# Routing by token tile, compression in column halves, and block 1's side work in another order

## The chip, the cores and the metric

The kernel runs on one core of a Trainium2 chip. The metric is the device time of one execution in microseconds (us); a profiled execution has its own time beside it. The engines are TensorE (PE, with its weight loads PEld), VectorE (DVE), ScalarE (ACT), GpSimd (POOL) and SyncE (SP), which issues most transfers.

## The reference, cut to what matters

The input x has 256 tokens of 1024 features. A first block and two further layers follow one another, all in float32.

```python
# block 1
h = rms_norm(x, g);  z = h @ w_in              # fox q,k,v,f; nsa q and keys/values; gates
out_a = fox_attention(q, k, v, log_sigmoid(f + b)) @ w_fox_up        # 8 heads of 64
kc, vc = gelu(blocks @ w1) @ w2                # compression of keys and of values, each its own w1, w2
out_b = nsa_attention(compressed, selected, window branches) @ w_nsa_up
x = x + (sigmoid(g_a) * out_a + sigmoid(g_b) * out_b) @ w_out
# experts: top group of 4, then top 2 of its 4 experts
t = rms_norm(x, g_ffn)
p_g, group = top_k(softmax(t @ w_group + b_group), 1)
top_p, top_i = top_k(softmax((t @ w_router + b_router)[group]), 2)
x = x + sum(w * (silu(t @ w_gate[e]) * (t @ w_up[e])) @ w_down[e])
# two layers: HGRN2 recurrence and sliding-window attention, post-norm, residual
for l in range(2): x = x + rms_norm(mixed(rms_norm(x, g_pre)) @ w_out_2[l], g_post)
```

## The kernel before, in words

Every large product is computed in float32r with both operands split into a high and a low part: three matmuls (`mm3`, hi*hi, hi*lo, lo*hi, the lines 507 to 509). Weights stream from memory in halves of 1 MB through a ring of four slots. Each half is four pieces of 512 columns; ScalarE writes a piece's high part (`feed`, line 1766), VectorE its low part (line 398), into nine buffers. PE eats two pieces per "take". Both engines run their feeds nine pieces ahead (`AHEAD`); a buffer is free when the take that used it has counted `taken`. Each engine runs its own written program, and semaphores with `wait_ge` join them. What an engine does besides the takes stands in a table by take number (`beside_block1`, `beside_layer`): a `step` is run by each engine `ahead` of or `behind` its part of the take.

Takes 0 to 23 compute z for block 1, four takes for 512 columns: tile a=0 of the tokens goes to bank 0, a=1 to bank 1. After each fourth take ScalarE copies bank 0 and VectorE bank 1 to `z3` (VectorE's line 1689), and PE's next take waits for both (`out_free`). In between run the head norms (`fox_sums`, `fox_norms`, `win_sums`, ...: VectorE squares and sums, GpSimd takes the root), the turns (transposes) of queries and keys (`fox_q`, `fox_k`, `nsa_side`), the forget gates (`forget`, whose end stands in VectorE's `fox_q`), and twelve attention jobs. A job has the steps scores, `scores_out` (VectorE mask and maxima, ScalarE exponentials), `weigh` (VectorE), turn, `turn_out`, values, `values_out`. Takes 24 to 39 are gates, 40 to 47 the up projections, 48 to 55 the output projection. Beside takes 28 to 42 run the thirteen steps of `compress`. Its steps 3 and 4 multiply keys' blocks and then values' blocks by w1 (line 711), each into partitions 0 to 63 of bank 7, 256 columns side by side; the four raw halves of w1 sit in the ring.

Takes 48 to 55 fill banks 4 to 7. Then VectorE adds the result to x, `norm(1)` squares (ScalarE, line 1780), takes the root (GpSimd), scales, PE turns x into feature rows with the gain applied on the way out (ScalarE and VectorE, eight copies each), and `route` computes 20 logits per token (`mm3` with 20 columns), softmax and choice of the group, ranks of tokens within their group (lines 786 to 790), eight selection matrices of 128 slots (`sel_r`), and the gather of each group's rows (line 805). If a group has more than 128 tokens, all engines but GpSimd run `full_pass`; the flag for it is read to a register by each engine (`value_load`, `If`), on PE ahead of the gather. In the run shown no group was so crowded. After the gather PE spreads the expert weights to slots (line 811), ScalarE and GpSimd split the rows (`expert_rows`), and 192 expert takes follow, 48 a group. `combine` adds the groups' results back, and the layers follow, with `pre_sum`, `pre_scale` and `pre_los` ahead of each and `y_sums`, `y_add` at its end.

Of the kernel before, what the change touches and what calls it, by code (L numbers as in the profile page):

```python
# [98 lines left out]
def weight_halves():  # L99
# [4 lines left out]
    for n in range(PN_CMP):  # L104
        for h in range(2):
            out.append((2 * n + h, PIECE if n != 2 else Z5, engines))
            if n == 8 and h == 1:
                out += [(2 * PN_CMP + i, 0, None) for i in range(2)]
            if n == 9 and h == 0:
                out += [(2 * PN_CMP + 2 + i, 0, None) for i in range(2)]  # L110
# [113 lines left out]
def build(nc, panels, x_in, prm_in, lay_in, pre_in, post_in, c0_in, c1_in, c2_in, out):  # L224
    ctx = ExitStack()
    with ctx:
# [96 lines left out]
        def sem(name):  # L323
# [12 lines left out]
            sem("norm_" + n) for n in ("sq", "ms", "rs", "x", "T", "hi", "lo"))  # L336
        x_new = sem("x_new")
# [4 lines left out]
        route_hi, route_lo = sem("route_hi"), sem("route_lo")  # L342
# [90 lines left out]

# [28 lines left out]
        full_x, full_w, full_g, full_hT = zin[:, 4096:5120], gates[:, :], buf_d[:, 1024:1536], buf_d[:, 1536:2048]  # L463
# [41 lines left out]
        def pe_program():  # L505
# [111 lines left out]
            def nsa_side(n):  # L617
                c, kind = SIDES[n]
                pe.wait_ge(heads_done, (3, 4, 3, 5)[n])
                if n == 0:  # L620
                    pe.wait_ge(norm_lo, 8)
                else:
                    pe.wait_ge(side, 5 + n)
                if kind == "q":
                    pair_turns(c, 7, z3).then_inc(side_T, 1)
                    return
                for a in range(TT):
                    i = turn128(ps[:, 7, a * P:(a + 1) * P], z3[:, a, c:c + P])
# [63 lines left out]
            def compress(step):  # L692
# [10 lines left out]
                elif step < 5:  # L703
                    c = step - 3
                    pe.wait_ge(cmp_blk, 8)
                    for h in range(2):
                        load = raw_at[2 * c + h]
                        pe.wait_ge(*landed(load))
                        w1 = ring[:, load % RING * HALF:(load % RING + 1) * HALF].rearrange("p (m n) -> p m n", m=8)
                        for n in range(8):  # L710
                            m = T.matmul(ps[0:64, 7, c * 256:(c + 1) * 256], blk[c][:, 8 * h + n, :, :].rearrange("p g n -> p (g n)"),  # L711
                                         w1[:, n, :], start=h == 0 and n == 0, stop=h == 1 and n == 7)
                elif step == 5:
                    pe.wait_ge(cmp_a, 1)
                    for i in range(4):
                        m = turn128(ps[:, 7, i * 64:(i + 1) * 64], scr[0:64, i * P:(i + 1) * P], 64)
                elif step == 6:
                    pe.wait_ge(cmp_v, 3)
                    pe.wait_ge(ld_prm, 16)
                    for c in range(2):  # L720
                        w2 = prmc(("w2_k", "w2_v")[c])
                        for i in range(2):
                            m = T.matmul(ps[0:64, 7, c * 64:(c + 1) * 64],
                                         scr[:, 512 + (2 * c + i) * 64:512 + (2 * c + i + 1) * 64],
# [51 lines left out]

            def route():
                pe.wait_ge(route_lo, 1)
                for a in range(TT):
                    for k in range(KT):  # L780
                        pe.wait_ge(norm_lo, 8 + k + 1)
                        m = mm3(ps[:, 0, a * 20:(a + 1) * 20], (hi3[:, k, a * P:(a + 1) * P], lo3[:, k, a * P:(a + 1) * P]),
# [3 lines left out]
                T.matmul(ps[:, 1, 0:4], ntri[:, 0:P], goh2[:, 0:4], start=True, stop=True)  # L786
                T.matmul(ps[:, 1, 4:8], ntri[:, P:2 * P], goh2[:, 0:4], start=True, stop=False)
                T.matmul(ps[:, 1, 4:8], ntri[:, 0:P], goh2[:, 4:8], start=False, stop=True)
                T.matmul(ps[:, 1, 8:12], ntri[:, P:2 * P], goh2[:, 0:4], start=True, stop=False)
                T.matmul(ps[:, 1, 8:12], ntri[:, P:2 * P], goh2[:, 4:8], start=False, stop=True).then_inc(rank_mm, 1)  # L790
# [6 lines left out]
                pe.wait_ge(chosen, 8)  # L797
                pe.wait_ge(rs_lo, 4)
                for k in range(KT):
                    if k >= 4:  # L800
                        pe.wait_ge(rows, k - 3)
                    b = 3 + k % 4
                    for x in (op_hi, op_lo):
                        for a in range(TT):
                            m = T.matmul(ps[:, b, :], x[:, a * D + k * P:a * D + (k + 1) * P], sel_r[:, a * 512:(a + 1) * 512],  # L805
                                         start=a == 0 and x is op_hi, stop=a == 1 and x is op_lo)
                    m.then_inc(row_mm, 1)
# [57 lines left out]
            def full_pass():  # L865
                for a in range(TT):
# [142 lines left out]
            for t in range(T_OUT, T_MOE):  # L1009
                k = t - T_OUT  # L1010
                pe.wait_ge(mix_lo, k // 2 + 1)
                out_take(t, op_rows, k, k == 0, k == KT - 1)
            norm_turns(1)
            route()
            for t in range(T_MOE, T_L2):
                expert(t)
                if t - T_MOE in SELECT_AT:
# [30 lines left out]
        def dve_program():  # L1048
# [49 lines left out]
            def fox_sums(n):  # L1098
                for a in range(TT):
                    dve.wait_ge(out_free[a], 2)  # L1100
# [1269 lines left out]
```

## Time and profile before

| what | us |
|---|---|
| median of 3 runs | 1128.57 (1127.06 to 1132.99) |
| the profiled execution | 1132.04 |
| its span, first to last instruction | 1130.2 |
| PE / VectorE / ScalarE / GpSimd busy | 1049.0 / 851.0 / 657.0 / 50.4 |
| mean granted clock of PE | 0.964 |

Busy times overlap, and PE counts as busy while matmuls are in its pipeline. The granted clock is 1.00 at 2.4 GHz and 0.50 at 1.2 GHz.

### The profile page before, as it was taken

The page shows a single profiled execution, that of the slowest core. Times are in us where ns is not written, and L with a number is a line of the kernel's source. Part 1 is how long each engine was busy: PE and PEld are TensorE (multiplying, and loading weights), DVE is VectorE, ACT ScalarE, POOL GpSimd, SP SyncE. Part 2 cuts the span into 40 slices and gives each one's busy share as a digit, 9 for nine tenths or more (in the row PEclk, how much of TensorE's full clock was granted, in tenths as well). Part 3 has the DMA queues.
Part 4 walks back from the last instruction along what each step waited for, and adds up shares of the span by engine and source line. Part 5 has one row for each costly group of instructions (what it writes and reads, how often), then busy time and mean ns, then how long its engine had stood idle before and what let it go on. Part 6 is the DMA issues. An engine that isn't in the chain of part 4 may idle for free.

```text
span 1130.2 us, 16492 instructions
## 1 busy us (share of the span) xinstructions
PE 1049.0 (93%) x6109; PEld 896.4 (79%) x6109; DVE 851.0 (75%) x1663; ACT 657.0 (58%) x1314; POOL 50.4 (4%) x44
## 2 busy tenths in 40 slices
PE   4898999897799999999989999999998999989997
PEld 4776878787588888887877898888876899978875
DVE  5666774674599999999986777697567877598673
ACT  5443545543488888888863566822345467653342
POOL 0201100000100101020000000000001000000010
PEclk9998999997699999999999999999998999999999
DMA  8422335242099999999973433323343533333320
GB/s 345 158 112 75 113 131 197 86 179 80 7 373 382 362 387 358 384 368 347 373 284 133 172 125 125 114 104 140 121 162 132 185 129 134 113 112 113 126 98 38
DMA packets 30036, 211.32 MB, mean 187 GB/s; under 512 B 3584, under 2 KB 3712, under 8 KB 4992
## 3 DMA queue, kind: packets, MB, share of 16 engines
q1 hardware_dynamic: 28368, 205.01, 48.8%
q10 hardware_dynamic: 1584, 5.20, 1.3%
q8 instruction: 52, 0.85, 0.3%
q14 instruction: 32, 0.26, 0.1%
HBM read 209.15 MB, written 1.05 MB: 186 GB/s over the span
## 4 chain that ended last, share of the span: by engine, by line
PE 64%; DVE 20%; ACT 7%; DMA 5%; issue 3%; POOL 0%; SPq 0%; DVEq 0%; POOLq 0%; ACTq 0%
PE ps L507 16%; PE ps L509 15%; PE ps L508 15%; DVE w_lo L398 9%; DMA ring<-in_panels 5%; PE ps L512 4%; PE ps L942 4%; PE ps L657 2%; ACT w_hi L1766 2%; PE ps L688 1%; PE ps L711 1%; ACT s_buf L1814 1%; DVE scr L398 1%; PE ps L805 1%; DVE op_lo L398 1%
## 5 line engine op out<-in xcount | busy, mean ns | idle before, releaser
L398 DVE TENSOR_TENSOR w_lo<-ring,w_hi 128x512 fp32r<-128x512 f32 x760 | 482.6, 689 | 108.8 <-ACT w_hi L1766 107.6
L1766 ACT ACTIVATE w_hi<-ring 128x512 fp32r<-128x512 f32 x760 | 426.2, 620 | 194.1 <-PE ps L509 161.8
L507 PE MATMUL ps<-w_hi,op_hi 128*128 128x512 f32 (+2 forms) x800 | 320.2, 400 | 19.5 <-ACT zin L1766 5.0
L509 PE MATMUL ps<-w_hi,op_lo 128*128 128x512 f32 (+2 forms) x800 | 312.9, 391 | 0.0
L508 PE MATMUL ps<-w_lo,op_hi 128*128 128x512 f32 (+2 forms) x800 | 312.4, 391 | 0.0
L507 PEld LDWEIGHTS ps<-w_hi,op_hi 128*128 128x128 f32 x800 | 154.2, 193 | 54.6 <-issue 10.4
L509 PEld LDWEIGHTS ps<-w_hi,op_lo 128*128 128x128 f32 x800 | 153.7, 192 | 31.6
L508 PEld LDWEIGHTS ps<-w_lo,op_hi 128*128 128x128 f32 x800 | 154.4, 193 | 28.0
L507 PE MATMUL ps<-op_hi,w_hi 128*128 128x256 f32 x544 | 157.5, 290 | 1.2 <-DVE op_lo L398 1.2
L508 PE MATMUL ps<-op_lo,w_hi 128*128 128x256 f32 x544 | 153.8, 283 | 0.0
L509 PE MATMUL ps<-op_hi,w_lo 128*128 128x256 f32 x544 | 153.7, 283 | 0.0
L507 PEld LDWEIGHTS ps<-op_hi,w_hi 128*128 128x128 f32 x544 | 104.0, 191 | 5.2 <-issue 2.5
L508 PEld LDWEIGHTS ps<-op_lo,w_hi 128*128 128x128 f32 x544 | 104.2, 191 | 0.0
L509 PEld LDWEIGHTS ps<-op_hi,w_lo 128*128 128x128 f32 x544 | 104.1, 191 | 0.0
L1814 ACT ACTIVATE s_buf<-s_buf,stat 128x256 f32<-128x256 f32 (+1 forms) x112 | 49.6, 444 | 73.2 <-DVE stat L401 73.2
L410 POOL TENSOR_TENSOR stat<-stat,minus_half 128x1 f32<-128x1 f32 (+5 forms) x20 | 25.9, 1296 | 842.8 <-DVE stat L404 842.8
L942 PEld LDWEIGHTS ps<-gates 128*128 128x128 f32 x448 | 54.3, 192 | 5.5 <-issue 3.3
L942 PE MATMUL ps<-gates 128*128 128x64 f32 x448 | 53.3, 271 | 3.0 <-DVE buf_c L1572 3.0
L512 PE MATMUL ps<-ident,scr 128*128 128x128 f32 (+3 forms) x109 | 18.9, 329 | 26.7 <-DVE scr L401 20.6
L512 PEld LDWEIGHTS ps<-ident,scr 128*128 128x128 f32 (+3 forms) x109 | 15.8, 170 | 29.3 <-issue 14.4
L1766 ACT ACTIVATE zin<-ps 128x512 f32<-128x512 f32 (+2 forms) x26 | 14.0, 554 | 38.6 <-PE ps L509 24.3
L398 DVE TENSOR_TENSOR gates<-gates,buf_d 128x512 f32<-128x512 f32 (+1 forms) x36 | 25.5, 746 | 13.3 <-PE ps L942 13.3
(244 smaller groups left out, 1131.2 us busy)
## 6 DMA issues: line engine op xcount, KB each, us to landing
ring<-in_panels SPq DMA_DIRECT2D x194, 1024.0 KB, 6.1
cst<-in_c ACTq DMA_DIRECT2D x1, 1219.0 KB, 5.4
buf_a<-in_pre ACTq DMA_DIRECT2D x2, 512.0 KB, 5.9
keys<-in_post ACTq DMA_DIRECT2D x2, 512.0 KB, 4.5
out<-x_tok SPq DMA_DIRECT2D x2, 512.0 KB, 2.6
cst<-in_c ACTq DMA_DIRECT2D x1, 960.0 KB, 7.0
x_tok<-in_x SPq DMA_DIRECT2D x1, 512.0 KB, 4.8
x_tok<-in_x ACTq DMA_DIRECT2D x1, 512.0 KB, 5.0
```

Of the source, the lines that this page charges most:

```text
L398: return V.tensor_tensor(o, a, b, op)
L410: return G.tensor_tensor(o, o, e.to_broadcast(list(o.shape)), ALU.pow)
L507: T.matmul(o, l[0], r[0], start=start, stop=False)
L508: T.matmul(o, l[0], r[1], start=False, stop=False)
L509: return T.matmul(o, l[1], r[0], start=False, stop=stop)
L512: return T.transpose(o, a, ident[0:n, 0:n])
L657: m = T.matmul(ps[:, 2 + e, lo:lo + n], q(a)[half, :], k[half, 0:n], start=True, stop=plain)
L688: m = T.matmul(ps[half, 6, kt * P:S], v3[:, kt, cc:cc + HD], pt[:, kt * S:S + kt * P], start=kt == 0, stop=kt == 1)
L711: m = T.matmul(ps[0:64, 7, c * 256:(c + 1) * 256], blk[c][:, 8 * h + n, :, :].rearrange("p g n -> p (g n)"), w1[:, n, :], start=h == 0 and ...
L942: m = T.matmul(ps[:, 2 + 2 * j + lv % 2, n * HD:(n + 1) * HD], k_of(j)[:, n * P:(n + 1) * P], late[:, n * per:(n + 1) * per, :], start=Tru ...
L1766: return A.activation(o, a, ACT.Copy, scale=scale)
L1814: i = A.activation(sc[:, lo:lo + n], sc[:, lo:lo + n], ACT.Exp, bias=ng_[:, c:c + 1], accum_out=sm[:, c:c + 1])
```

## The change

- `last_takes_1`: the last four output takes run all of tile a=0 and then all of a=1. Squares, root, scaling, turns, splitting and logits are done per tile. The gain `g_ffn` is multiplied into the router's weights once (in `lower`), so that the turned rows need none. The rows to be gathered are split from `scr` into `pick_hi`, `pick_lo`.
- In `route`, the group's sum and reciprocal come after its choice; ranks take two products; the gather starts at four selections and goes through four banks for a=0 and then a=1. ScalarE copies rows and splits expert rows in turn. The branch comes behind the gather on PE and ScalarE. The slot weights move behind the third expert take, their copy behind the fifth.
- VectorE feeds pieces 115 to 118 inside `route`, behind the selections.
- Compression: steps 3 and 4 each take a half of w1 for keys and values, keys to partitions 0 to 63 and values to 64 to 127. Step 8 is cut in two (`cmp_weigh`), and the weighings of jobs 7 and 11 come ahead (`weigh_now`).
- Block 1: new places in the table; bank copies ahead of the feed (VectorE) and ahead of the exponentials (ScalarE); `forget` ends in VectorE's `fox_k`; `nsa_side` 1 uses bank 3.
- `combine` and tails: tile a=0 is summed and scaled ahead of a=1's sums; mean and epsilon come from one instruction; one feed stands ahead of the combine.

```diff
-    table = {4: [("lower", 0)], 9: [("fox_sums", 0)], 10: [("fox_sums", 1)], 11: [("fox_norms", 0), ("forget", 0)],
-             12: [("fox_norms", 1), ("fox_q", 0), ("nsa_gates", 0)], 13: [("fox_k", 0)],
-             20: [("win_sums", 0)], 21: [("win_norms", 0), ("nsa_side", 0)], 22: [("nsa_side", 1)],
+    table = {3: [("lower", 0)], 5: [("fox_sums", 0)], 7: [("fox_norms", 0)], 9: [("fox_sums", 1), ("fox_q", 0)],
+             11: [("fox_norms", 1), ("forget", 0)], 12: [("fox_k", 0), ("nsa_gates", 0)],
+             20: [("win_sums", 0)], 21: [("win_norms", 0)], 22: [("nsa_side", 0), ("nsa_side", 1)],
...
+    for take, job in ((31, 7), (39, 11)):
+        table[take].remove(("weigh", job))
+    table[30].insert(table[30].index(("compress", 2)), ("weigh_now", 7))
+    table[38] += [("weigh_now", 11), ("cmp_weigh", 0)]
...
+                    for n in range(8):
+                        for c in range(2):
+                            m = T.matmul(ps[c * 64:(c + 1) * 64, 7, 0:256],
+                                         blk[c][:, 8 * h + n, :, :].rearrange("p g n -> p (g n)"),
+                                         w1[c][:, n, :], start=h == 0 and n == 0, stop=h == 1 and n == 7)
...
+            def last_takes_1():
+                for a in range(TT):
+                    for k in range(KT - 4, KT):
+                        w = weights_of(T_MOE - KT + k)
+                        pe.wait_ge(mix_lo, k // 2 + 1)
+                        for h in range(2):
+                            m = mm3(ps[:, 4 + 2 * a + h, :], op_rows(k, a), w[h], False, k == KT - 1)
+                        if a == 1:
+                            m.then_inc(taken, 1)
+                    if a == 0:
+                        m.then_inc(ffn_mm, 1)
...
+                for a in range(TT):
+                    for c in range(2):
+                        pe.wait_ge(ffn_x, 2 * a + c + 1)
+                        for i in range(4):
+                            o = a * D + (4 * c + i) * P
+                            m = turn128(ps[:, 2 + 2 * a + c, i * P:(i + 1) * P], scr[:, o:o + P])
+                        m.then_inc(ffn_T, 1)
                     for k in range(KT):
-                        pe.wait_ge(norm_lo, 8 + k + 1)
+                        pe.wait_ge(ffn_lo, 2 * a + k // 4 + 1)
...
+                for k0 in (0, 4):
+                    for a in range(TT):
+                        pe.wait_ge(chosen, 4 * (a + 1))
+                        for k in range(k0, k0 + 4):
+                            if k0 and a == 0:
+                                pe.wait_ge(rows, k - 3)
+                            for y in (pick_hi, pick_lo):
...
                 pe.wait_ge(flagged, 1)
                 more = T.value_load(flag[0:1, 0:1], min_val=0, max_val=S)
                 with T.If(more > 0):
...
+            ffn_sum(0)
+            ffn_scale(0)
+            feed(2 * (T_MOE - 3) + AHEAD)
+            ffn_sum(1)
+            ffn_lo_(0)
+            ffn_scale(1)
+            pick_los(0)
+            ffn_lo_(1)
+            pick_los(1)
             route()
```

## Rows read from the trace of the kernel before

**Rows 1.** Windows by stage: length, busy us (instructions) of each engine, clock, DMA share, GB/s

```profile
264.43:307.11 42.68, 28.05 (x122) 25.74 (x123) 18.96 (x72) 17.59 (x33) 1.56 (x3) 0.60 0.02 4
307.11:587.65 280.54, 280.20 (x1255) 229.53 (x1256) 266.87 (x427) 238.27 (x443) 19.20 (x15) 0.99 0.96 365
```

**Rows 2.** Timeline, PE in block 1: start, us, instruction [idle before <-releaser]

```profile
51.37 0.80 PE L507 MATMUL ps<-w_hi,op_hi 128*128 128x512 f32 x1 [3.62 <-DVE zin L1689]
...
71.09 0.47 PE L507 MATMUL ps<-w_hi,op_hi 128*128 128x512 f32 x1 [2.49 <-ACT zin L1766]
...
109.45 0.48 PE L512 MATMUL ps<-ident,zin 128*128 128x128 f32 x1 [2.30 <-DVE zin L398]
...
156.21 0.87 PE L512 MATMUL ps<-ident,s_buf 128*128 128x128 f32 x6 [2.49 <-DVE s_buf L401]
...
211.57 1.40 PE L512 MATMUL ps<-ident,s_buf 128*128 128x128 f32 x6 [2.66 <-DVE s_buf L401]
```

**Rows 3.** Windows, the stretch behind the first hole

```profile
51.33:54.74 3.41, 3.37 (x10) 2.69 (x11) 1.55 (x4) 1.73 (x4) 1.75 (x1) 0.50 0.00 0
```

**Rows 4.** Timeline, VectorE and ScalarE in the fox stage

```profile
47.06 1.21 DVE L398 TENSOR_TENSOR scr<-zin 128x1024 f32<-128x1024 f32 x1
...
50.87 0.44 DVE L1689 COPY zin<-ps 128x288 f32<-128x288 f32 x1
...
55.28 0.69 DVE L398 TENSOR_TENSOR w_lo<-ring,w_hi 128x512 fp32r<-128x512 f32 x1 [2.33 <-ACT w_hi L1766]
...
53.22 1.28 ACT L1794 ACT_TABLE_LOAD   x1
```

**Rows 5.** Timeline, VectorE behind the maxima of the first job

```profile
68.48 1.28 DVE L398 TENSOR_TENSOR w_lo<-ring,w_hi 128x512 fp32r<-128x512 f32 x2
69.68 0.68 DVE L1689 COPY zin<-ps 128x512 f32<-128x512 f32 x1
```

**Rows 6.** Groups by form (busy us, mean ns), and a timeline row of the value products

```profile
L711 PE MATMUL ps<-ring,buf_d 128*64 128x256 f32 x64 | 15.2, 399 | 0.0
...
188.15 0.87 PE L688 MATMUL ps<-pt_buf,zin 128*64 128x256 f32 x8
```

**Rows 7.** Timeline, VectorE ahead of the weighings of jobs 7 and 11

```profile
152.62 2.21 DVE L398 TENSOR_TENSOR buf_d<-buf_c,prm 128x120 f32<-128x120 f32 x8
...
208.07 0.69 DVE L1333 TENSOR_REDUCE stat<-scr 128x16 f32<-128x512 f32 x1 [0.70 <-ACT scr L1873]
```

**Rows 8.** Windows, the products with 20 columns and the gather's first part

```profile
274.29:284.33 10.04, 10.03 (x47) 9.93 (x47) 1.77 (x5) 2.13 (x4) 0.00 (x0) 0.50 0.01 2
294.64:300.50 5.86, 5.86 (x14) 4.62 (x15) 2.26 (x15) 3.02 (x4) 0.00 (x0) 0.50 0.02 6
```

**Rows 9.** The chain that ended last, in the routing: start, us, what

```profile
289.70 0.15 DVE flag L1392
289.85 2.06 DVE sel_r L401 x8
291.91 2.73 issue
...
294.64 10.37 PE ps L805 x32
```

**Rows 10.** Timeline, the routing

```profile
264.45 2.48 DVE L398 TENSOR_TENSOR x_tok<-x_tok,ps 128x512 f32<-128x512 f32 x4 [0.76 <-PE ps L509]
...
270.60 3.67 PE L512 MATMUL ps<-ident,scr 128*128 128x128 f32 x16 [6.18 <-DVE scr L401]
...
296.12 1.28 ACT L1766 ACT_TABLE_LOAD   x1 [3.17 <-issue]
...
304.83 1.85 PE L811 MATMUL ps<-stat,sel_r 128*128 128x16 f32 x16
```

**Rows 11.** Timeline, PE at the head of the first layer

```profile
590.71 1.97 PE L512 MATMUL ps<-ident,scr 128*128 128x128 f32 x8 [2.66 <-DVE scr L1651]
...
602.76 0.47 PE L507 MATMUL ps<-w_hi,op_hi 128*128 128x512 f32 x1 [2.26 <-DVE w_lo L398]
```

More of the change, by code:

```diff
@@ L796, in route, with weights_by_slot @@
                     pe.seen = seen
[L797 to L807, printed above, removed]
+            def weights_by_slot():
                 pe.wait_ge(weights, 2)
@@ L865, in full_pass @@
             def full_pass():
+                pe.wait_ge(rows, KT)
                 for a in range(TT):
@@ L1392, in route @@
                 V.tensor_copy(flag[:, 0:1], most).then_inc(flagged, 1)
-                dve.wait_ge(own, 1)
-                for i in range(8):
-                    ts(sel_r[:, i * P:(i + 1) * P], c1("slot"), rank[:, i:i + 1], goh2[:, i:i + 1], ALU.is_equal,
-                       ALU.mult).then_inc(chosen, 1)
                 dv(tt(pg, gm, gr, ALU.mult))
@@ L1667, in dve_program, with steps @@
                      "head_scale": head_scale}
-            def ahead(t):
+            def steps(t):
                 for name, arg in beside.get(t, ()):
@@ L1672, in ahead @@
                         table[name](arg)
+            def ahead(t):
+                steps(t)
                 feed(2 * t + AHEAD)
@@ L1682, in dve_program @@
             for t in range(T_Z, T_GATE):
-                ahead(t)
+                steps(t)
                 i, step = divmod(t, 4)
@@ L1720, in dve_program @@
                 expert_out(t)
+            feed(2 * T_L2 + AHEAD)
             combine()
@@ L1901, in route @@
                     act.seen = seen
-                for k in range(KT):
-                    act.wait_ge(row_mm, k + 1)
-                    copy(rin[:, k, :, :], ps[:, 3 + k % 4, :].rearrange("p (g n) -> p g n", g=4),
-                         prmc("g_ffn", k, k + 1)).then_inc(rows, 1)
             def hidden_hi(e):
@@ L2004, in act_program, with steps @@
                      "compress": compress, "cross": cross, "hgrn_values": hgrn_values, "hg_turn": hg_turn}
+            def steps(t, *names):
+                for name, arg in beside.get(t, ()):
+                    if name in names:
+                        table[name](arg)
             def ahead(t):
                 feed(2 * t + AHEAD)
-                for name, arg in beside.get(t, ()):
-                    if name in ("turn_out", "scores_out"):
-                        table[name](arg)
+                steps(t, "turn_out", "scores_out")
             def behind(t):
@@ L2026, in act_program @@
             for t in range(T_Z, T_GATE):
-                ahead(t)
+                feed(2 * t + AHEAD)
+                steps(t, "turn_out")
                 i, step = divmod(t, 4)
@@ L2053, in act_program @@
                 behind(t)
-            for t in range(T_OUT, T_MOE):
+            for t in range(T_OUT, T_MOE - 3):
                 feed(2 * t + AHEAD)
-            norm(1, [(x_new, 2), (x_new, 4)])
+            ffn_square(0)
+            feed(2 * (T_MOE - 3) + AHEAD)
+            ffn_his(0)
+            ffn_square(1)
+            pick_his(0)
+            ffn_his(1)
+            pick_his(1)
+            feed(2 * (T_MOE - 1) + AHEAD)
             route()
-            for h in range(4):
-                expert_rows(0, h)
             for t in range(T_MOE, T_L2):
```

270 lines of the change are left out of this document (172 added, 98 removed).

## The prediction

> **What bounds the kernel now.** I read the windows by stage first, then TensorE's (PE's) own rows for its idle stretches, then the chain of waits through the routing. The expert stage (307.11 to 587.65) is full: PE is busy 280.20 of 280.54 us at a clock of 0.99, VectorE 266.87, the transfers 0.96 of their share [rows 1]. Nothing in the change takes work out of it. The routing stage (264.43 to 307.11) is the opposite: 42.68 us at a mean clock of 0.60, no transfers, each engine waiting for another [rows 1]. Block 1 and the two layers are PE-bound with single holes. PE's rows give them with their releasers: 3.62 us behind a bank copy, 2.49 behind another (its twin at 95.01 has 2.46), 2.30 behind head norms, 2.49 and 2.66 behind a weighing [rows 2]. Each is followed by 3.41 us at clock 0.50, as the first [rows 3]: what PE does in such a stretch takes double, so a hole costs itself and up to 1.7 us.
>
> So the sum is made hole by hole. It is made against the profiled execution (span 1130.2, execution 1132.04) and then taken off the median of the runs, 1128.57, which lies 3.5 below that execution.
>
> **Fox heads sooner (takes 3 to 13): loss 2.9.** Before, the copy of bank 1 stood behind two head sums and a feed, and PE waited until 50.87 + 0.44 [rows 4]. Now the first sums stand in take 5, and VectorE, with one square and one reduction of 1.2 us for each sum, has 1.5 us free per take of 2.72; but the second sums, `fox_q`'s two scalings and two feeds still lie between take 9 and the copy. I get the copy at about 50.4 with PE there at 48.0: the hole shrinks to 2.4. What is late next is `forget`. Its chain runs VectorE (0.6), ScalarE with a table load of 1.28 between two activations, and ScalarE's next weight copies queue behind it: VectorE waited 2.33 for them [rows 4]. Before, PE asked for the forget gates after take 13, a take later. Now PE's `fox_k` stands behind take 12, and VectorE finishes `forget` only behind its feed in take 12, which waits for those ScalarE copies. Step by step: forget_x 53.4, log 55.15, copies 56.3, feed 57.0, forget 57.4, while PE's eight turns are done at 53.7. PE idles 3.7, runs a slow stretch after it (1.5), and gets to the first scores at about 65.4, where it was at 62.6. Bounds: 4.6 lost if both holes bring a slow stretch; 5.3 gained if the old hole and its stretch simply go.
>
> **Bank copies ahead of the exponentials and the feed; nsa_side 0 a take later: gain 9.7.** Before, VectorE fed 1.28 behind its maxima and then copied 0.68 [rows 5], and ScalarE copied only behind all exponentials, which let PE go at 71.09 [rows 2]. Now ScalarE copies during the take and VectorE right behind the maxima (68.5 to 69.2), while PE is still on the a=0 half of take 16. Holes of 2.49 and 2.46 and the 2.30 behind the norms go, with a slow stretch each (1.7): 12.35. Against it: VectorE's feed and weighing come later against a faster PE, and turns wait for weighing instead: I count 0.7, 0.2, 0.2 and 0.8 after takes 16, 20, 22 and 25, with 0.8 of smaller ones. Bounds: nothing gained net (every hole moves into `weigh`), and 12.4.
>
> **Compression (takes 30 to 34): gain 9.65.** Steps 3 and 4 were 64 instructions, 15.2 us, 0.22 each at full clock [rows 6]. The edit sends k to output partitions 0 to 63 and v to 64 to 127 in turn. The value products already do that: 8 instructions, two pairs of 256 columns and two of 128, took 0.87 [rows 6]; one after the other at 0.22 and 0.11 they would take 1.3. So pairs run together, and each step should take 3.55: 2 x 3.5 saved. The other 2.65 come from `weigh_now 7` ahead of the 2.21 us of block sums [rows 7]: the hole of 2.49 becomes 0.75 before the turns and 0.4 before the products, and the slow stretch behind it goes. Bounds: no overlap, then only 2.65; both in full, 10.5. The Trainium skill ("TensorEngine Tiling (Array Packing)", Key Properties) says that changing the tiling mode drains the engine, which speaks against mixing modes. The trace shows about 0.2 at such borders, and here their number stays, so the sum stays.
>
> **`weigh_now 11` ahead of half of step 8: gain 2.75.** The chain that starts at 208.07 [rows 7] and fills 2.1 us moves behind the weighing, which is then done at 208.8, as values(10) ends. Turns for the compressed scores wait 1.1 instead. I count no slow stretch behind a hole this short. Bounds: 1.5 and 3.9.
>
> **Routing by token tile: gain 12.0 up to the first expert product.** In times of the old trace:
> - The last four takes run a=0 first, so its sums are ready at 259.0, 5.44 before the end. Adding to x (2.48 for both tiles), squares, root and scaling filled 264.45 to 270.60 for both [rows 10]; for one tile I take 4.2, done at 263.2, hidden. PE turns a=0 at 264.45 without the wait it had until 270.60 [rows 10]. ScalarE copy, VectorE remainder: first products at 266.4.
> - 48 products with 20 columns take 0.213 each at half clock (274.29 to 284.33) [rows 8]. The clock stayed at half under them, although PE was never idle in them, so I take full clock only until about 268. a=0 ends at 269.8, turns for a=1 271.6, remainders 272.8, products end at 277.1 instead of 284.33: 7.2. Bounds: half clock throughout 279.2, full 273.5.
> - Sum and reciprocal leave the path (0.27), ranks take 2 products instead of 5 (0.43 each): gather starts after the fourth of eight selections (8 took 2.06 [rows 9]), at 281.6 instead of 294.64: 13.0 so far. VectorE's feed of four pieces (2.45), pushed behind the selections, makes the second exponential late (287.5), which costs ScalarE a copy slot but PE nothing.
> - Gather: 10.37 before, at half clock until 300.50 [rows 8, 9]; I take 10.0, ending 291.6.
> - The branch. Before, it took 4.8 from the flag (289.70 + 0.15) to 294.64, of which 2.06 lay beside the selections and 2.73 showed in the chain [rows 9]. Behind it, the expert rows' splitting took 2.1 from the end of the gather to 307.11. Now that splitting lies beside the gather, and nothing but the queue lies beside PE's branch. ScalarE's own took 3.17, up to its table load [rows 10]; I take that, since PE's sequencer may start while the last products run: first expert product at 294.8, so 12.3, rounded to 12.0 for ScalarE's table load (1.28) now behind its branch. Bounds 0 and 4.75 for the branch.
>
> **`weights_by_slot` into the expert stage: loss 1.6.** Its 16 products (1.85 [rows 10]) lay beside the splitting; now they lie in a stage without a hole. Bounds 0 (transfers limit there) and 2.7 (the first reload comes 0.8 later as well).
>
> **Between the stages: gain 4.9.** Feeding two pieces ahead of the combine removes the 2.26 before 602.76 (weights of the fourth take). a=0's root and scaling ahead of a=1's sums would bring the turns at 590.71 forward by 2.1, but ScalarE still squares a=1 before it copies a=0, so 0.8 arrives [rows 11]. The tails lose two tiny steps and put the root ahead of one 0.65 us product: 1.1 between the layers, 0.7 at the end. Bounds 2 and 7.
>
> **Sum:** -2.9 + 9.7 + 9.65 + 2.75 + 12.0 - 1.6 + 4.9 = 34.5. Execution 1132.04 - 34.5 = 1097.5; median 1128.57 - 34.5 = **1094**.
>
> **Rivals.**
> - Column halves one after the other: 7.0 less, 1101. Only the pairs of rows 6 speak against it; those are short. 0.10.
> - The branch costs PE all of 4.75 and the clock stays at half through the gather (0.2 for each of 18 products): 1.6 + 3.6 less, 1099. For it: the clock rose only 5.9 us into the old gather [rows 8]. 0.15.
> - The branch is free: 3.2 more, 1091. 0.10.
> - The fox stage doesn't lose: if `forget` is early enough and the copy too, 8.2 more, 1086. 0.10.
> - The holes only move: VectorE, with the same work before each weighing, makes PE wait in `weigh` what it waited in the copies: 9.7 and 2.65 less, 1106. 0.10.
> - Slower: VectorE becomes the bound of the expert stage. It was busy 266.87 of 280.54, 1.39 us of each take's 1.46. It enters the stage with its branch and two pieces still ahead, where it had idled 9.4 us. If it adds 0.2 us to each of 192 takes, 38 us are lost and the time is about 1133. It decides from 5% more VectorE time per take; nothing in the edits adds that, and a backlog of two pieces (1.3 us) is worked off. 0.02.
>
> The forecast itself has 0.43. Of two measurements about 0.5% (5.6 us) can be told from none. All cases but the last, and a rest of several shortfalls together, are beyond it: faster 0.95, same 0.03, slower 0.02. Range: 1084 (fox stage and branch both good, with little else lost) to 1107 (holes only move).
>
> **What would show it.** PE's 3.62 hole gone or shrunk to 2.4 and a new one of 3 to 4 us behind the fox turns, before products of 8 columns. No holes at the two copies. Products of L711's kind in pairs, 3.5 us a step. The 20-column products in two runs, the second ending about 13 us after the last output take. The gather without a gap after the selections, then 0 to 4.75 us of nothing before the first expert product, some 30 us after that last take. Expert stage within 2 us of 280.5. Wrong would be: block 1 gaining under 10 us, or an expert stage above 284.

## The result and the profile after

The changed kernel takes 1097.32 us (median of 4, 1095.85 to 1098.28) against 1128.26 for the kernel before: ratio 0.9717, 95% interval 0.9687 to 0.9747. Its profiled execution took 1097.71, with a span of 1095.7. One execution of a later version (the best of the above) took 1444 us at a mean clock of 0.655; its row in the table below leaves it out.

The windows of the changed kernel: from the last output take to the first expert product, the half-clock stretch in it, and the expert stage to the combine's last product. Columns as in [rows 1].

```profile
245.45:275.29 29.84, 22.30 (x103) 18.59 (x101) 19.79 (x72) 15.62 (x29) 2.76 (x4) 0.71 0.11 37
250.10:267.16 17.06, 12.87 (x51) 11.43 (x51) 10.78 (x34) 5.80 (x10) 0.00 (x0) 0.50 0.06 13
275.29:558.90 283.61, 281.95 (x1273) 229.99 (x1274) 267.96 (x432) 237.95 (x447) 17.36 (x14) 1.00 0.95 364
```

The last output take ends at 245.5 instead of 264.4, and the routing takes 29.84 instead of 42.68 [rows 1]. The expert stage takes 283.6; before, it was 280.9 by the same marks (307.11 to 588.04), so it is 2.7 longer.

PE's idle stretches in the changed kernel's timeline, to be held against [rows 2, 4]:

```profile
50.14 0.51 PE L519 MATMUL ps<-w_hi,op_hi 128*128 128x512 f32 x1 [1.19 <-DVE zin L1779]
52.47 1.09 PE L524 MATMUL ps<-ident,zin 128*128 128x128 f32 x8 [0.66 <-DVE zin L405]
56.98 0.57 PE L625 MATMUL ps<-stat,cst 128*128 128x8 f32 x2 [3.42 <-DVE stat L405]
...
147.85 0.88 PE L524 MATMUL ps<-ident,s_buf 128*128 128x128 f32 x6 [0.86 <-DVE s_buf L408]
149.98 3.67 PE L725 MATMUL ps<-ring,buf_d 128*64 128x256 f32 x32 [0.39 <-DVE buf_d L405]
```

The hole of 3.62 at the copy is down to 1.19, and `forget` costs 3.42 at the products of 8 columns. The holes at the later copies are gone. Compression's step of 32 products takes 3.67. The same timeline in the routing, for [rows 9, 10]:

```profile
245.56 1.03 PE L524 MATMUL ps<-ident,scr 128*128 128x128 f32 x8
247.70 0.28 PE L519 MATMUL ps<-wr_hi,op_hi 128*128 128x20 f32 x1 [1.10 <-DVE op_lo L405]
...
253.22 0.39 PE L519 MATMUL ps<-wr_hi,op_hi 128*128 128x20 f32 x1 [0.56 <-DVE op_lo L405]
...
260.65 0.60 PE L819 MATMUL ps<-stat,cst 128*128 128x8 f32 x2 [2.13 <-DVE stat L1454]
...
263.18 1.19 PE L829 MATMUL ps<-sel_r,zin_r 128*128 128x512 f32 x2 [1.50 <-DVE sel_r L408]
...
275.29 0.47 PE L519 MATMUL ps<-w_hi,op_hi 128*128 128x512 f32 x1 [1.95 <-POOL op_lo L2289]
```

Turns start as the last take ends. The last hole is put down to GpSimd's low part, but the weight load of that product has "2.34 <-issue": it waited for nothing that the profile shows. Of GpSimd's low parts the product needs only the first, and that was done at 270.40 by GpSimd's timeline:

```profile
269.67 0.73 POOL L2289 TENSOR_TENSOR op_lo<-gates,op_hi 128x256 fp32r<-128x256 f32 x1 [20.53 <-ACT op_hi L1864]
```

What stands between the gather and that product in PE's program is the branch. A run below takes it out.

### The profile page after: what moved, and what is told of

Same layout as the page of the kernel before. It is cut to its first block, busy times and chain, and to the rows that moved or that the text cites. A ratio compares the mean times of both kernels' runs of the same rounds, so it can differ in the third digit from the quotient of the medians.

```text
span 1095.7 us, 16470 instructions
## 1 busy us (share of the span) xinstructions
PE 1029.7 (94%) x6101; PEld 880.1 (80%) x6101; DVE 849.1 (77%) x1657; ACT 651.8 (59%) x1310; POOL 48.6 (4%) x45
## 4 chain that ended last, share of the span: by engine, by line
PE 54%; DVE 24%; ACT 10%; DMA 7%; issue 3%; POOL 0%; SPq 0%; DVEq 0%; POOLq 0%; ACTq 0%
PE ps L519 14%; PE ps L521 13%; PE ps L520 13%; DVE w_lo L405 12%; DMA ring<-in_panels 7%; PE ps L977 4%; PE ps L524 3%; ACT w_hi L1864 3%; PE ps L670 2%; PE ps L701 1%; ACT s_buf L1912 1%; DVE s_buf L408 1%; DVE op_lo L405 1%; DVE scr L405 1%; DVE zin L1692 1%
## 5 line engine op out<-in xcount | busy, mean ns | idle before, releaser
L1912 ACT ACTIVATE s_buf<-s_buf,stat 128x256 f32<-128x256 f32 (+1 forms) x112 | 49.6, 445 | 64.3 <-DVE stat L408 64.3
L524 PE MATMUL ps<-ident,scr 128*128 128x128 f32 (+2 forms) x107 | 17.5, 310 | 18.6 <-DVE scr L408 14.3
L524 PEld LDWEIGHTS ps<-ident,scr 128*128 128x128 f32 (+2 forms) x107 | 13.9, 157 | 21.3 <-issue 15.6
```

The lines of the kernel that those rows point to most:

```text
L524: return T.transpose(o, a, ident[0:n, 0:n])
L1912: i = A.activation(sc[:, lo:lo + n], sc[:, lo:lo + n], ACT.Exp, bias=ng_[:, c:c + 1], accum_out=sm[:, c:c + 1])
```

## Experiments

All runs: median, lowest and highest time, and the ratio to before with its 95% interval.

| run | us | ratio |
|---|---|---|
| forget's end early | 1095.98 (1093.17 to 1097.70) | 0.9713 (0.9649 to 0.9777) |
| and keys in take 13 | 1093.44 (1092.95 to 1095.02) | 0.9700 (0.9638 to 0.9762) |
| fox stage in the old order | 1094.96 (1093.97 to 1099.30) | 0.9720 (0.9655 to 0.9786) |
| tile 0's copies first | 1097.21 (1095.87 to 1098.20) | 0.9730 (0.9667 to 0.9792) |
| no branch | 1093.76 (1092.39 to 1094.82) | 0.9682 (0.9623 to 0.9742) |
| fillers | 1099.27 (1098.62 to 1100.97) | 0.9735 (0.9675 to 0.9795) |
| column halves alone | 1121.94 (1117.82 to 1126.27) | 0.9932 (0.9901 to 0.9962) |
| copies alone | 1126.58 (1123.54 to 1131.43) | 0.9980 (0.9950 to 1.0011) |
| no feed ahead | 1098.91 (1097.95 to 1099.64) | 0.9725 (0.9688 to 0.9761) |
| before again | 1127.93 (1125.18 to 1134.98) | 0.9988 (0.9962 to 1.0014) |
| best of the above | 1090.50 (1088.25 to 1092.52) | 0.9657 (0.9624 to 0.9690) |
| and keys beside the spreading | 1088.85 (1085.23 to 1090.29) | 0.9663 (0.9639 to 0.9686) |

The ratios rest on before's scatter (1121.5 to 1136.2 in its executions beside these runs), so variants are compared by their times and their traces. The median of the kernel before lay between 1127.6 and 1130.1 beside the different groups of runs. A difference of 2 us or less between two versions is therefore not shown by the times alone. The changed kernel itself has 1097.32 and 0.9717.

**Forget's end ahead of the feed.** `forget_end` is what stood first in VectorE's `fox_k`.

```diff
-             12: [("fox_k", 0), ("nsa_gates", 0)],
+             12: [("forget_end", 0), ("fox_k", 0), ("nsa_gates", 0)],
...
-                    if name in ("weigh", "scores_out", "qf_bound"):
+                    if name in ("weigh", "scores_out", "qf_bound", "forget_end"):
```

> The changed kernel, with the end of forget (VectorE, two instructions) ahead of its feed in take 12 instead of behind it. In the changed kernel PE waits 3.42 us (53.56 to 56.98) for it, since VectorE first waits 2.33 for ScalarE's copies. Theory (forget is what is late, and VectorE's place in the queue makes 1.9 of it): forget ends at about 55.0, the hole shrinks to 1.4 to 1.6, the first scores come at about 63.9 instead of 65.81, and if the slow stretch behind the hole goes too, at 62.2. Time 1095.4, or 1093.7 without the slow stretch. Rival (ScalarE's table loads and copies set it): the hole stays above 3 and the time at 1097.3.

PE's timeline behind the turns of keys:

```profile
56.33 0.36 PE L625 MATMUL ps<-stat,cst 128*128 128x8 f32 x2 [1.70 <-DVE stat L405]
```

The hole halves; half clock lasts 3.4 us instead of 6.8. The first scores come at 64.3, although in this execution the first rise of the clock came 2.2 later than in the changed kernel's. The rival is out by the trace. The time is 1.3 lower, which does not decide; the expert takes were the longest of all profiles (277.45 against 276.16).

**Keys in take 13.**

```diff
-             12: [("fox_k", 0), ("nsa_gates", 0)],
+             12: [("forget_end", 0), ("nsa_gates", 0)], 13: [("fox_k", 0)],
```

> As the run with the end of forget ahead of the feed, and fox_k one take later (13, as in the kernel before). Theory: PE asks for forget after take 13 and finds it ready; no hole behind the turns of keys, and no slow stretch from it; 3.42 and up to 1.7 go: first scores at 60.7 to 62.4 instead of 65.81, time 1092.2 to 1093.9. Rival (only the slow stretch moves, because the hole of 1.19 at the bank copy brings it too): first scores at 62.4, time 1093.9. Second rival (VectorE's key copies, now a take later, make the first scores wait): first scores at 64 or later, time above 1095.

PE's timeline at the first scores:

```profile
61.96 0.49 PE L670 MATMUL ps<-keys,buf_a 64*128 64x256 f32 x2 [1.95 <-DVE stat L408]
```

There is no wait for `forget`, PE has full clock from the first rise to the end of block 1, and the time is 1093.44 as expected. But there is a new hole of 1.95 ahead of the first scores.

**The fox stage in the old order.**

```diff
-    table = {3: [("lower", 0)], 5: [("fox_sums", 0)], 7: [("fox_norms", 0)], 9: [("fox_sums", 1), ("fox_q", 0)],
-             11: [("fox_norms", 1), ("forget", 0)], 12: [("fox_k", 0), ("nsa_gates", 0)],
+    table = {4: [("lower", 0)], 9: [("fox_sums", 0)], 10: [("fox_sums", 1)], 11: [("fox_norms", 0), ("forget", 0)],
+             12: [("fox_norms", 1), ("fox_q", 0), ("nsa_gates", 0)], 13: [("fox_k", 0)],
```

> The changed kernel with the fox stage in the order of before: sums in takes 9 and 10, norms in 11 and 12, queries in 12, keys in 13, the end of forget and GpSimd's spreading with the queries; the bank copies stay ahead of the feed. It prices the term that was forecast at a loss of 2.9. Theory (the new order loses what it wins at the copy and more at forget): the hole at the copy is 1.5 to 2.4, no wait for forget, first scores at 61.5 to 62.9 instead of 65.81, time 1093 to 1094.5. Rival (the new order is worth its hole, and the copy would be late again at 3.6 as before): first scores at 65 or later, time 1097 or above.

PE's timeline, the hole at the bank copy and the first scores:

```profile
50.23 0.50 PE L519 MATMUL ps<-w_hi,op_hi 128*128 128x512 f32 x1 [2.41 <-DVE zin L1779]
...
62.64 0.70 PE L670 MATMUL ps<-keys,buf_a 64*128 64x256 f32 x4 [0.26 <-DVE stat L408]
```

The first scores are 3.2 earlier than with the new order (65.81): by the trace the new order of the fox stage is a loss in the changed kernel. The time is 2.4 lower, but the ratios are equal (0.9720 and 0.9717), so the times don't decide it.

**Tile 0's copies first.**

```diff
                     pre_squares(0, 0)
-                    pre_squares(0, 1)
                     pre_his(0, 0)
+                    pre_squares(0, 1)
                     pre_his(0, 1)
```

> The changed kernel; at the head of the first layer ScalarE copies the turned rows of tile 0 ahead of squaring tile 1. The forecast said that only 0.8 arrives there because ScalarE squares first. In the changed kernel PE waits 2.61 us (until 562.68) with 3.4 at half clock behind it. Theory: the copies start at 559.5 instead of 561.23, first product of the layer at 561.0 to 561.3, hole 1.0 to 1.2; 1.5 gained, or 3.2 if the slow stretch goes too. Time 1095.8 or 1094.1. Rival (VectorE's sum into x for tile 1 stands ahead of its remainders and is late): first product at 562 or later, 0.5 gained at most.

PE's timeline at the first product of the layer:

```profile
563.13 0.47 PE L519 MATMUL ps<-w_hi,op_hi 128*128 128x512 f32 x1 [1.23 <-DVE op_lo L405]
```

The hole falls from 2.61 to 1.23, and no half clock follows it: from the combine's end to PE's last product it is 527.5 instead of 530.0. Whether the smaller hole did away with the half clock is open: of seven profiles with the hole of 2.6 at this place, two (no branch, no feed ahead) have none behind it either. The time doesn't show it (0.1 lower). Its profiled execution had lost 1.7 before the first scores, where both programs are the same. By the time alone this run is inconclusive.

**No branch**: `value_load`, `If` and `full_pass` are taken out on three engines.

> The changed kernel without the branch for crowded groups on PE, VectorE and ScalarE (the pass for groups over 128 tokens is left out; the input has none). Forecast: the branch costs 3.2 visible behind the gather; in the trace PE idles 1.95 between gather and first expert product. Theory: PE's own branch is the whole hole: first expert product some 1.5 to 1.95 sooner, time 1095.4 to 1095.8. Rival one (the wait is for the split rows anyway, and the branch is free): the same within 0.3. Rival two (the branches of ScalarE and VectorE, 3.2 and 7, delay weight pieces later on and cost as well): 3 us or more, 1094 or below.

PE's timeline, the gather's last products and the first of the experts:

```profile
273.78 0.85 PE L829 MATMUL ps<-sel_r,zin_r 128*128 128x512 f32 x3
...
274.46 0.39 PE L519 MATMUL ps<-w_hi,op_hi 128*128 128x512 f32 x1
```

No hole is left: from the gather's start to the first expert product it is 10.2 us instead of 12.1, so all of the 1.95 went with the branches. Of the three, only PE's own stands ahead of that product: its first weights and low parts were ready. The time is 3.6 lower, as rival two had it. The other 1.6 are partly seen (expert takes 0.6 shorter, no half clock at the layer's head behind the same hole of 2.61), but both lie within what equal programs differ by and are not shown to be the branch's.

**Fillers.** Products whose result nobody reads, four ahead of the ranks and three ahead of the gather:

```diff
+                for _i in range(4):
+                    T.matmul(ps[:, 7, :], hi3[:, 0, 0:P], op_hi[:, 0:512], start=True, stop=True)
                 pe.wait_ge(own, 1)
```

> The changed kernel with seven products of 512 columns whose results nobody reads, in PE's two waits of the routing: four ahead of the ranks (hole 2.13) and three ahead of the gather (hole 1.50). They add no time of their own if they fit. PE is granted half clock from 250.10 to 267.16, through the gather's first 4 us. Theory (the half clock comes from what PE did in the 20-column stretch and its holes, and fuller work brings it back sooner): full clock from the gather's start, gather 8.2 to 8.5 instead of 10.2, 1.5 to 2 gained, time 1095.5. Rival (the clock comes back no sooner, or the gather waits for ScalarE's row copies instead): gather ends within 0.5 of 273.34, time 1097.3, or 0.5 more if the fillers overrun.

PE's timeline in this run:

```profile
258.95 2.05 PE L819 MATMUL ps<-op_hi 128*128 128x512 f32 x4
261.24 0.60 PE L821 MATMUL ps<-stat,cst 128*128 128x8 f32 x2 [0.23 <-DVE stat L1458]
261.69 0.57 PE L822 MATMUL ps<-stat,cst 128*128 128x8 f32 x2
262.12 1.63 PE L824 MATMUL ps<-op_hi 128*128 128x512 f32 x3
```

Its window over the half-clock stretch, columns as in [rows 1]:

```profile
251.08:268.15 17.07, 16.26 (x56) 13.22 (x56) 10.93 (x38) 5.80 (x10) 0.00 (x0) 0.50 0.08 28
```

PE was busy 16.26 of 17.07 us and was granted half clock all the same, as long as without fillers; the gather took 10.18. The theory is out: fuller work did not bring the clock back sooner. The routing is as long as without fillers (29.50 and 29.57, from the end of the last output product to the first expert product). The time is 1.9 higher; the trace shows expert takes 1.0 longer (277.2), and the fillers are not shown to be the cause.

**Column halves alone**, in the kernel before: the compression's part of the change.

> The kernel before, with the compression in column halves alone (steps 3 to 6 and the order of the raw halves of w1). Theory: the 64 products fall from 15.1 to 7.3 us as pairs of rows run together, and nothing else in block 1 moves: the first take behind step 4 comes 7 to 7.8 sooner, time 7 to 7.8 below the kernel before. Rival (in the changed kernel the pairs are fast, but elsewhere a wait takes up what they free, the weighing of job 8 or the raw halves' transfers): 4 or less gained, with a new hole between takes 31 and 35.

Its group by form, for [rows 6]:

```profile
L712 PE MATMUL ps<-ring,buf_d 128*64 128x256 f32 x64 | 7.3, 382 | 0.0
```

PE's timeline behind the unchanged weighing:

```profile
154.21 0.87 PE L512 MATMUL ps<-ident,s_buf 128*128 128x128 f32 x6 [2.49 <-DVE s_buf L401]
155.87 3.67 PE L712 MATMUL ps<-ring,buf_d 128*64 128x256 f32 x32
```

15.2 [rows 6] became 7.3, and the time is 6.8 below before's 1128.70 (19 executions beside this run). But "nothing else in block 1 moves" did not hold in this profile. Block 1 ends 11.3 sooner than before (253.1 for 264.4): 7.8 by the products, and the rest because four holes that were followed by half clock before were not here. These are the windows behind the holes of 2.49 (ahead of the turns above) and of 2.31 (behind the head norms), columns as in [rows 1]:

```profile
154.20:157.70 3.50, 3.49 (x32) 2.58 (x34) 2.84 (x6) 1.33 (x2) 0.00 (x0) 1.00 0.00 0
...
108.90:112.40 3.50, 3.42 (x18) 2.84 (x18) 3.05 (x10) 0.90 (x2) 0.00 (x0) 1.00 0.00 0
```

Holes of the same size (2.49 and 2.30) had 3.41 us of half clock behind them in the first profile of before. The time did not keep all of the 11.3: the expert takes were 2.1 longer (275.6).

**Copies alone**, in the kernel before: the two loops over takes 0 to 23.

```diff
             for t in range(T_Z, T_GATE):
-                ahead(t)
+                steps(t)
...
                     V.tensor_copy(z3[:, 1, n * 512:n * 512 + cols], ps[:, 1, 0:cols]).then_inc(out_free[1], 1)
+                feed(2 * t + AHEAD)
```

> The kernel before, with the bank copies ahead of the feed (VectorE) and ahead of the exponentials (ScalarE) alone; table and forget as before. Theory: the hole of 3.62 at take 12 shrinks by VectorE's feed of 1.28 to 2.3, the holes of 2.49 and 2.46 at the later copies go, with a slow stretch each, 1.3 + 2 x 4.1 less 1 to 2 of weighing that comes later: 6.5 to 8.5 gained. Rival (the holes only move into the weighing, since VectorE has the same work before it): 2 or less gained.

PE's timeline, the turns of jobs 0 and 2 and the first of `nsa_side`, for the second to fourth row of [rows 2]:

```profile
72.46 0.87 PE L512 MATMUL ps<-ident,s_buf 128*128 128x128 f32 x6 [1.02 <-DVE s_buf L401]
...
93.38 0.88 PE L512 MATMUL ps<-ident,s_buf 128*128 128x128 f32 x6 [0.17 <-DVE s_buf L401]
...
102.79 1.12 PE L512 MATMUL ps<-ident,zin 128*128 128x128 f32 x4 [2.57 <-DVE zin L398]
```

The two holes became 1.02 and 0.17 at the turns, and block 1 ended 5.8 sooner. The hole behind the head norms stayed (2.57); it takes `nsa_side` in take 22 as well. The time is 2.1 below before's 1128.70, which is less than before's scatter: the trace speaks for the mechanism, the times decide nothing, and the 6.5 to 8.5 of the forecast are not shown. Against the second profile of before (below), block 1 ends 6.4 sooner, but the routing takes 42.5 instead of 38.0: there PE had half clock for 30.7 us instead of 23.9.

**No feed ahead**: `feed(2 * T_L2 + AHEAD)` left out on both engines.

> The changed kernel without the two pieces that VectorE and ScalarE feed ahead of the combine and the first layer. Forecast: this feed removes the hole of 2.26 us at the fourth take of the layer. Theory: a hole of 2.2 to 2.3 comes back behind the turns of tile 1 (in the changed kernel PE goes on there at 569.26), the head of the layer starts no sooner, since nothing else stood in front of the combine; 2.3 lost: 1099.6. Rival (the feed ahead only moves the wait: it delays the first product of the layer, and without it that hole of 2.61 shrinks by VectorE's 1.28): 1.3 of it comes back, time 1098.3 or below.

PE's timeline at the head of the first layer, for [rows 11]:

```profile
564.00 0.47 PE L519 MATMUL ps<-w_hi,op_hi 128*128 128x512 f32 x1 [2.61 <-DVE op_lo L405]
571.50 0.47 PE L519 MATMUL ps<-w_hi,op_hi 128*128 128x512 f32 x1 [2.27 <-DVE w_lo L405]
```

The old hole is back (2.27 for 2.26), and the one ahead of it didn't shrink. The time is 1.6 higher, less than the 2.3 forecast. In the trace the way from the combine's end to PE's last product is only 0.5 longer (530.6): this execution had one half-clock stretch less in the layers.

**Before again**, unchanged.

> The kernel before once more, unchanged, for a second profile of it. The profiled execution of before took 3.5 us over its median, and the traces' difference of 34.5 us is that much above the medians' 30.9. In seven profiles of the changed kernel and its variants the same program reached the same place up to 1.7 us apart before the first scores (the first rise of the clock comes between 17.4 and 20.3), and the expert takes from 274.2 to 277.5 us long. Theory (such scatter makes the 3.5, mostly in block 1, where each of before's holes can bring a half-clock stretch or none): this span lies 2 to 4 us under 1130.2, with fewer or shorter half-clock stretches in block 1, or fewer in the routing; expert takes within 273 to 276. Rival (the first profile is typical and profiling itself adds it): the span is 1129 to 1131 again.

Its windows: routing, expert stage, and the products with 20 columns.

```profile
265.02:303.01 37.99, 23.71 (x122) 21.67 (x123) 18.93 (x72) 17.25 (x33) 1.56 (x3) 0.69 0.01 4
303.01:582.71 279.70, 278.60 (x1256) 228.52 (x1256) 266.19 (x427) 237.55 (x443) 17.94 (x15) 1.00 0.96 366
...
274.46:281.80 7.34, 7.34 (x50) 7.24 (x48) 2.12 (x6) 2.44 (x5) 0.00 (x0) 0.73 0.01 3
```

The span is 1125.3, 4.9 less instead of 2 to 4, and the theory placed most of it wrongly: block 1 ended 0.6 later than in the first profile, with as much half clock. The routing is 4.7 shorter with the same instructions. The same 20-column products ran at clock 0.73 and took 7.34 instead of 10.04 [rows 8]. That is 2.7 of it. Another 1.25 lies between the gather's start and the first expert product (11.22 for 12.47, at clock 0.86 for 0.76), 0.4 ahead of the 20-column products and 0.3 between those and the gather.

**The best of the above**: `forget_end` early, keys and `nsa_gates` in take 13, tile 0's copies first.

> The changed kernel with the end of forget ahead of VectorE's feed, keys in take 13, nsa_gates (ScalarE, a table load) in take 13 as well, and tile 0's copies ahead of tile 1's squares at the head of the first layer. With the first two alone the time was 1093.44, with a new hole of 1.95 ahead of the first scores, where VectorE's key copies stood behind four low parts that waited for ScalarE (its table load for nsa_gates, 1.28, in front). Theory: that hole shrinks to under 0.8 and 1.4 to 1.5 come at the layer's head, as in its own run: time 1090.3 to 1091.0. Rival (what is gained ahead of the expert stage is lost in it, since its transfers are at 0.97 and the takes scatter by 3 us): 1092 to 1093.5.

The time is 1090.50, in the theory's range, but not for its reason: the hole did not shrink. It stayed at 1.96, with ScalarE's table load out of the way. PE's timeline at the first scores, then VectorE's:

```profile
62.10 0.70 PE L670 MATMUL ps<-keys,buf_a 64*128 64x256 f32 x4 [1.96 <-DVE stat L408]
...
56.48 2.37 DVE L405 TENSOR_TENSOR w_lo<-ring,w_hi 128x512 fp32r<-128x512 f32 x1
...
60.57 1.40 DVE L408 TENSOR_SCALAR keys<-ps,prm 128x512 f32<-128x512 f32 x2
```

GpSimd's, in the same time:

```profile
56.40 1.89 POOL L2275 COPY buf_d<-stat 128x2048 f32<-128x2048 f32 x1 [5.00 <-DVE stat L405]
```

The first of four low parts came up 0.08 after GpSimd's spreading had started and took 2.37; the others took about 0.68. That points to VectorE being held up by GpSimd, which the next run puts to the test.

**Keys beside the spreading.**

```diff
-             12: [("forget_end", 0)], 13: [("fox_k", 0), ("nsa_gates", 0)],
+             12: [("forget_end", 0), ("fox_k_out", 0)], 13: [("fox_k", 0), ("nsa_gates", 0)],
```

Here `fox_k_out` is VectorE's part of `fox_k`, ahead of its feed.

> As the run before it (forget's end early, keys in take 13, tile 0's copies first), with one thing moved: VectorE's scaling of the keys comes right behind forget's end, ahead of its feed in take 12. In that run the hole of 1.96 ahead of the first scores stayed, though ScalarE's table load had gone from its place: VectorE's first low part started at 56.48, just behind GpSimd's spreading (56.40 to 58.30), and took 2.37 instead of 0.68, while the key scalings of the changed kernel, which read their tile from PSUM, ran beside that spreading in 0.75 and 0.74. Theory (the two engines exclude each other where VectorE reads two tensors of SBUF, and it is this that makes the keys late): the scalings take 0.75 each beside the spreading, the next low part starts behind it and takes 0.7 to 1.0, the hole is under 0.5, the first scores come 1.5 to 1.9 sooner, time 1089.5 to 1090. Rival (VectorE simply has too much to do ahead of the scores): the hole moves to the next take, which waits for its low parts; time 1091.4.

VectorE's timeline:

```profile
56.03 1.40 DVE L408 TENSOR_SCALAR keys<-ps,prm 128x512 f32<-128x512 f32 x2
57.35 0.16 DVE L408 TENSOR_SCALAR stat<-ps 128x16 f32<-128x16 f32 x1
57.44 1.18 DVE L405 TENSOR_TENSOR w_lo<-ring,w_hi 128x512 fp32r<-128x512 f32 x1
```

GpSimd's:

```profile
56.18 1.89 POOL L2275 COPY buf_d<-stat 128x2048 f32<-128x2048 f32 x1 [5.00 <-DVE stat L405]
```

The scalings ran beside the spreading unharmed, and the next low part waited for its end: 1.18, done 0.55 behind it. The first scores follow at 59.84 without a hole, 2.3 sooner. At 1088.85 this version takes 3.4% less than the kernel before and 8.5 us less than the changed one (about 6 by the ratios). It is 1.7 below the version ahead of it, which the times alone do not show.

## Why the prediction was right, and where it was off

The time was forecast at 1094 and is 1097.3, in the range. The span fell by 34.5, the sum as worked out. That exactness is partly luck: the terms are off by up to 1.1 and their errors cancel, and against the second profile of before the span falls by 29.6 only. In the order of the list below the traces give -3.2, +10.0, +9.7, +2.5, +12.8 (with the branch), -2.7 and +5.4.

- **Fox stage, -2.9: right.** The first scores come at 65.81 instead of 62.56, -3.2. The mechanism (`forget` behind VectorE's feed, which waits for ScalarE) and the hole (3.7 forecast, 3.42 measured) are confirmed by three runs. With the old order the first scores come 3.2 sooner (0.3 of it from an earlier start). Two sizes were off and cancel: the hole at the copy is 1.19, not 2.4, and the half clock lasted 6.8 us instead of 3.4.
- **Copies and `nsa_side`, +9.7: right.** From the first scores to the turns of job 6 the traces differ by 9.98 (82.45 to 72.47). The rival that the holes only move into `weigh` is out: 1.02, 0.17, 0.66 and 0.84 stand there. But 5.1 of the forecast are three stretches of half clock, "with a slow stretch each", and what before pays for those is not fixed: in the profile of the column halves alone, two of the three holes had none, and the same way took 79.3. Against that execution the gain is 6.9.
- **Compression, +9.65: right.** From the turns of job 6 to those of job 9 it is 43.9 before and 34.2 after. Pairs run together. The rival with serial halves is out. The part for `weigh_now 7` has its holes right (0.86 and 0.39 for 0.75 and 0.4). Its sum is less clear: 2.49 - 1.15 and a slow stretch of 1.7 make 3.0, where the prediction has 2.65, and the same holds for the next term (2.66 - 1.1 + 1.7 is 3.3, not 2.75). The prediction gives no reason.
- **`weigh_now 11`, +2.75:** 2.3 up to the values behind it and 2.5 to the end of block 1, with holes of 1.11 and 0.75 in the place of 2.66.
- **Routing, +12.0:** 12.8 against the first profile, but 8.2 (37.99 to 29.84) against the second. The timeline of the changed kernel was forecast well: the first expert product 30.4 after the last output take (294.8 - 264.43), and 29.8 measured. Here it is the other side of the difference that went wrong. The step "48 products with 20 columns take 0.213 each at half clock" took one execution's clock for the program's. The changed kernel ran them at half from 250.10 on. What before pays in the routing differs between its two profiles by 4.7 us, of which those products are 2.7.
- **The branch, 3.2 visible:** the hole was 1.95, and all of it went with the branch. The rival of 4.75 is out; the free branch (0) too. The Trainium skill's queue of 64 for TensorE ("Advanced Engine Details and Errata", Engine Queue Depths) would have hidden it altogether. The trace doesn't agree. PE's last wait ahead of the branch, for the fourth row copy, ends at 270.75, and the first expert product comes 4.54 later, about the 4.8 that the old branch took from flag to gather. That fits a sequencer that starts on the branch once its last wait is past and overlaps it with the 2.6 us of products still queued; no run isolates this.
- **Expert stage, -1.6:** -2.7. The slots' 16 products take 1.85. The rest lies within the scatter and has no shown cause: nine profiles of the changed kernel and its variants with a branch had takes of 274.2 to 277.5 us, four profiles of the kernel before and its variants 272.2 to 275.6, and in the changed kernel's profile PE has four holes of 0.23 to 0.48 behind low parts. Close to three of them ScalarE waited 0.27 to 0.38 for a transfer into the ring; close to the fourth, a low part of VectorE beside GpSimd's took 1.22. The stage moves 364 GB/s at a share of 0.95.
- **Between the stages, +4.9:** from the combine's end to PE's last product 534.3 became 530.0, 4.3, and another 1.0 comes behind that product, where 0.7 was forecast: 5.4 in all.

So the step that was off is the last line of the sum: "median 1128.57 - 34.5". The profiled execution lay 3.5 over its median, and the working carried a gain measured against it over to the median whole. A part of that gain, in the routing, was this execution's own excess. The spans of the second profile and the changed kernel differ by 29.6, the medians by 30.9. The rule under the sum, "a hole costs itself and up to 1.7 us", keeps its "up to": the same holes came with the half clock in one execution of the same code and without it in another.

## What to carry to other kernels

A hole's price must be read from more than one execution where the clock changes state. Take a second profile before a sum is made against the first. When an early step is late, ask in which queue its last small instructions stand: two of 0.17 us behind a feed made PE wait 1.7 us longer than ahead of it. Where a stage streams weights at the limit of the transfers, what is gained ahead of it can be lost in its scatter (takes of 272.2 to 277.5 here), and only the traces show where.

## What the runs showed of the hardware

- VectorE and GpSimd exclude each other for some operations only. A subtraction of two SBUF tensors took 2.37 and 1.18 instead of 0.68 us when it came up during GpSimd's copy, and ended 0.56 and 0.55 behind that copy's end. A scaling that read its tile from PSUM took 0.7 beside it. The Trainium skill ("SBUF — State Buffer", SBUF: two separate sides) states this: a VectorE operation with two SBUF inputs and a GpSimd operation that reads SBUF take the ports they share as an exclusive lock, for a whole instruction. The traces agree, and the GpSimd copy here does read SBUF (`stat`).
- A PE busy 95% of a stretch with 20-column and then 512-column products was still granted half clock for 17.07 us, as long as with 75% (12.87 of 17.06). Other versions without fillers had 17.1 or 20.5 us of it in the same place.
- After the same holes PE was granted half clock for 3.41 us in some executions and not in others: behind all six (2.3 to 3.6 us long) holes of block 1 in both profiles of before, behind two of the six in the column halves' profile.
- Column halves of 64 run side by side: 64 products of 256 columns took 7.3 us, 0.114 each, where one half alone took 15.2.
